# Eight of the 24 table units that are turned beside the first feed-forward's output product are turned later, beside the query product

## The reference: two transformer blocks, the second ending in a layer of single experts

```python
def swiglu(x, w_gu, w_down):                      # first_block, ffn1 (d_ff = 2816)
    g, u = jnp.split(x @ w_gu, 2, axis=-1)
    return (jax.nn.silu(g) * u) @ w_down
...
h = h + 0.5 * rmsnorm(swiglu(rmsnorm(h, ffn1_pre_w), ...), ffn1_post_w)
...
def peer(h, p):                                   # the last layer of second_block
    q = (hf @ p['peer_w_q']).reshape(T, 8, 2, 128)
    s = jnp.einsum('thpd,hpnd->thpn', q, p['peer_keys'])
    top_s, top_i = lax.top_k(s, 16)               # and again over the 256 sums
    ...
    act = jax.nn.gelu(jnp.einsum('td,thkd->thk', xb, u_tab[ib]))
    return jnp.einsum('thk,thkd->td', gb * act, v_tab[ib])
```

## Time and profile before

| | us |
|---|---|
| median of 3 runs | 3853.92 (3853.06 to 3856.65) |
| span of the profiled execution | 3844.7 |
| the execution around its span (median less span) | 9.2 |
| TensorE busy in the span | 3560.4 (93%) |
| VectorE busy | 2403.7 (63%) |
| ScalarE busy | 1320.1 (34%) |
| GpSimd busy | 1860.2 (48%) |
| TensorE in the stretch 460:480 | 9.5 of 20 |

### The profile page before, as it was taken

How to read it: one execution, slowest core, us unless ns; L and a number is a source line. 1 busy time by engine, 2 the same in 40 slices (tenths; PEclk the granted TensorE clock), 3 DMA queues, 4 the chain that set the end, 5 groups by cost and what they waited for, 6 DMA issues and landing times. The chain is left out here.

```text
span 3844.7 us, 49787 instructions
## 1 busy us (share of the span) xinstructions
PE 3560.4 (93%) x17547; PEld 3013.0 (78%) x17547; DVE 2403.7 (63%) x4244; ACT 1320.1 (34%) x1795; POOL 1860.2 (48%) x909
## 2 busy tenths in 40 slices
PE   8999897899999899978989899899999999989998
PEld 5777676677787688765667577689999999988898
DVE  4653255422324454156763754569999996999997
ACT  4332234232343322222323344323345553332332
POOL 5766333233244344331334112346566666788775
PEclk9999998999999999988999999999999999999999
DMA  6997944345366365231324223785469998988895
GB/s 245 392 384 258 297 150 136 116 155 173 120 225 223 101 192 170 89 100 59 116 77 137 71 66 107 230 314 166 156 228 351 343 349 292 344 327 342 327 339 196
DMA packets 458130, 813.81 MB, mean 212 GB/s; under 512 B 31544, under 2 KB 308984, under 8 KB 455322
## 3 DMA queue, kind: packets, MB, share of 16 engines
q1 hardware_dynamic: 278416, 436.07, 34.4%
q10 hardware_dynamic: 142666, 241.11, 17.8%
q0 software_dynamic: 36864, 134.23, 9.3%
HBM read 682.84 MB, written 195.56 MB: 228 GB/s over the span
## 5 line engine op out<-in xcount | busy, mean ns | idle before, releaser
L530 POOL TENSOR_TENSOR weights_lo<-weights_raw,weights_hi 128x1024 fp32r<-128x1024 f32 x649 | 1600.3, 2471 | 1913.8 <-ACT weights_hi L1204 1725.8
L606 PE MATMUL bank<-operand_hi,weights_hi 128*128 128x512 f32 (+1 forms) x2856 | 1093.1, 383 | 64.1 <-DVE operand_lo L1885 23.0
L608 PE MATMUL bank<-operand_hi,weights_lo 128*128 128x512 f32 (+1 forms) x2856 | 1063.8, 372 | 0.0
L607 PE MATMUL bank<-operand_lo,weights_hi 128*128 128x512 f32 (+1 forms) x2856 | 1063.5, 372 | 0.0
L1204 ACT ACTIVATE weights_hi<-weights_raw 128x1024 fp32r<-128x1024 f32 x649 | 681.7, 1055 | 828.3 <-PE bank L608 646.2
L606 PEld LDWEIGHTS bank<-operand_hi,weights_hi 128*128 128x128 f32 x2856 | 541.2, 190 | 156.8 <-DVE operand_lo L1885 29.1
L607 PEld LDWEIGHTS bank<-operand_lo,weights_hi 128*128 128x128 f32 x2856 | 541.4, 190 | 74.4 <-issue 6.1
L608 PEld LDWEIGHTS bank<-operand_hi,weights_lo 128*128 128x128 f32 x2856 | 540.4, 189 | 74.9
L606 PE MATMUL bank<-expert_hi,weights_hi 128*128 128x384 f32 x1024 | 356.6, 348 | 51.3 <-DVE expert_lo L2557 49.1
L607 PE MATMUL bank<-expert_lo,weights_hi 128*128 128x384 f32 x1024 | 352.4, 344 | 0.0
L608 PE MATMUL bank<-expert_hi,weights_lo 128*128 128x384 f32 x1024 | 352.0, 344 | 0.0
(11 more groups left out here) (399 smaller groups left out, 5061.7 us busy)
## 6 DMA issues: line engine op xcount, KB each, us to landing
weights_raw<-in_w_ffn_gu SPq DMA_DIRECT2D x132, 512.0 KB, 5.3
expert_table_v<-in_w_peer_out SPq DMA_DIRECT2D x120, 512.0 KB, 5.3
weights_raw<-in_w_peer_ahead SPq DMA_DIRECT2D x120, 512.0 KB, 3.9
weights_raw<-in_w_peer_out SPq DMA_DIRECT2D x120, 512.0 KB, 4.4
expert_table_u<-expert_turned ACTq DMA_DIRECT2D x288, 128.0 KB, 4.4
expert_rows<-in_w_peer_ahead ACTq DMA_DIRECT2D x64, 512.0 KB, 6.2
peer_gates<-gate_stage SPq DMA_DIRECT2D x24, 1024.0 KB, 8.9
expert_gates<-peer_gates ACTq DMA_DIRECT2D x16, 1536.0 KB, 12.1
```

Source lines behind the costliest of these rows:

```text
L530: pool.tensor_tensor(LO[:, slot, :], RAW[:, slot, :], HI[:, slot, :].bitcast(F32), ALU.subtract).then_inc(sem("lo_ready"), 1)
L606: pe.matmul(out, wh, hi(k), start=(k == 0), stop=False)
L607: pe.matmul(out, wh, lo(k), start=False, stop=False)
L608: ins = pe.matmul(out, wl, hi(k), start=False, stop=(k == kc - 1))
```

## The change

The ranges of `TABLE` move: d1 has 16 units instead of 24, q has 40 instead of 32 (so 31 instead of 23 in wq, since wout2 keeps nine), f2 keeps 18. `DOWN_TURNS` says how many turns stand before each of the eight blocks of d1: 3, 3, 3, 3, 2, 2, 0, 0. ScalarE's wait for the last stores of d1 moves from before the eighth square to behind the root. The total number of turns, loads and stores stays 128, 128 and 512.

```diff
-TABLE = {"f1": range(0, 54), "d1": range(54, 78), "f2": range(78, 96), "q": range(96, 128)}
+TABLE = {"f1": range(0, 54), "d1": range(54, 70), "f2": range(70, 88), "q": range(88, 128)}
 WOUT_TURNS = 9
+DOWN_TURNS = [3, 3, 3, 3, 2, 2, 0, 0]
+assert sum(DOWN_TURNS) == len(TABLE["d1"])
@@ scalar, ffn
                     if name == "ffn1":
-                        for _ in range(3):
+                        for _ in range(DOWN_TURNS[m]):
                             save_rows("d1")
                     square(YT[:, m, :], TOK, "block_free", n["freed"] + m + 1)
-                    if name == "ffn1" and m == DC - 1:
-                        for i in range(2):
-                            act.wait_ge(sem(f"table_stored_d1{i}"), 64 * len(TABLE["d1"]) // 2)
@@ scalar, after ffn1
             ffn("ffn1", n["freed"], x_squares)
             root(TOK)
+            for i in range(2):
+                act.wait_ge(sem(f"table_stored_d1{i}"), 64 * len(TABLE["d1"]) // 2)
@@ vector, ffn
-                        for t in range(3 * m, 3 * m + 3):
+                        for t in range(sum(DOWN_TURNS[:m]), sum(DOWN_TURNS[:m + 1])):
                             turn_rows("d1", t)
                         copy_blocks(YT, 1, FC, first=m, scaled=True)
```

## The result

Median 3862.9 us over 8 runs (3856.9 to 3869.3), against 3853.3 over 8 runs of the kernel before on the same chip (3849.8 to 3856.7): the medians differ by 9.6 us, the ratio is 1.003 with a 95% interval of 1.002 to 1.004 (7.7 to 15.4 us). So the changed kernel is slower, by about a quarter of a percent. The prediction said 3864.6, in 3849 to 3874.

What follows compares the result with a forecast made beforehand. TensorE was busy in 3560.4 of 3844.7 us, so changes matter where it stands still or is made to; -8.8 + 17 + 2.5 = +10.7 us on 3853.9 gave 3864.6, range 3849 to 3874.

Steps and rivals of the forecast that it cites:

- First term: End of d1: copies of blocks 6 and 7 wait for TensorE alone, reciprocal earlier; gain 8.8 us, range 7.8 to 9.8.
- Second term: wq: eight added turns wait for rows at the DMA rate, last query copy later; cost 17 us, range 12 to 22.
- The catch-up of four turns: wq before the change: four late turns took 12.92 us, 3.23 us each; called the forecast's weakest point.
- rival 1: wq: the q stage keeps up and only the d1 gain is left, 3845.1 us, faster; chance 0.13.
- Third term: Score products behind wq: TensorE idles some 17 us, then runs at the lower clock; cost 2.5 us, bounds 0 and 4.
- Nothing absorbs it: Behind wq: TensorE and VectorE both begin behind the last query copy, so neither can catch up the 17 us.
- The sum: Whole kernel: -8.8 + 17 + 2.5 = +10.7 us, median 3864.6 us.
- The 9.2 us: Whole kernel: median of runs 3853.92 less span 3844.7, taken to lie outside the span and kept unchanged.
- Two of the signs: Reciprocal of d1 8 to 10 us earlier; last query copy some 8 us later on the clock of the span.
- About a fifth: Share of the forecast's 0.59 (wq cost under 14 us) ending under 3861.6 us, so counted as no change.
- rival 3: wq: the f1 stage's lower rate of 359 GB/s holds, wq cost 28.8 us, time 3876.4 us; chance 0.07.
- The estimate that I drew from it: wq: by the skill page's bound of about 358 GB/s a core, the wq cost would be 27 us.

Runs made afterwards that it cites:

- d1_only: Changed kernel with q's units as before, so eight units are copied unturned (output not the reference's): 3839.4 us, 12 us under before.
- wait_only: Kernel before with only the wait for d1's stores moved behind the root, three turns left beside each block: no change that can be measured.
- q_only: Kernel before with 40 units in q instead of 32, eight being turned twice: 3874.5 us, 22 us above before by the medians.
- six_buffers: Changed kernel with six row buffers in q instead of four: 3859.9 us.
- half_rows: Changed kernel loading only 512 of 1024 columns of q's rows from number 13 on (output not the reference's): 3858.4 us.
- sp_half: Changed kernel with q's row loads from number 13 on issued by SyncE behind its weight loads, and halved (output not the reference's): 3852.1 us.
- sp_loads: Changed kernel with q's row loads from number 13 on issued by SyncE behind its weight loads, at full size: 3866.3 us.

## Why the prediction was right, point by point

**First term (-8.8).** Right, for the reason given: d1_only and wait_only show that the turns did 8 of the 10 us. The term's chain had one row too many: I left the root's table load (1.28 us) on the path, and it moved ahead of the mean. So the chain became 10.0 us shorter, just outside my 7.8 to 9.8. The 8.75 us of the pair of traces lie inside it by luck: TensorE lost 1.3 us within d1 in that one execution (from the first copy to the last matmul 109.8 us, in before 108.5; the granted clock over 345 to 470 was 0.97, in d1_only 0.99), in d1_only it lost nothing, and the gain in A is 10.0 us. Over all seven kernels with 16 turns A is 112.7 us on average, against 122.5, 122.1 and 120.9 in the three with turns up to block 7 (before, q_only, wait_only). TensorE's wait for weights within d1 is no part of it (3.1 us before, 3.0 after). The lower clock behind it lasted 3.9 us as before (483.56 to 487.47).

**Second term (+17).** The mechanism was right, the size low: 19.9 us, inside my 12 to 22. The ends of that range were worked loosely: by the same sum 430 GB/s gives 12.9 us and 3.4 us a turn 20.8; 19.9 lies between these too. A turn took 3.37 us, not 3.23. The catch-up of four turns had no weaker moment in it; over the whole stage the rate by bytes is 34.6 MB in 87.6 us, 395 GB/s, as single turns waited longer (4.80 us between those at 2496.24 and 2501.04). The ceiling itself was as read, 402 to 404 GB/s. In the rivals I had also held the ring of row buffers (3.1 us a turn) against rival 1; six_buffers and the 2.52 us a turn of sp_half with four buffers show that the ring isn't what held the turns. And I had counted ScalarE's issuing for rival 1 (5.4 of 5.5 us); half_rows shows that it takes 6.0 us a block, so that without the ceiling rival 1 would have failed too, on ScalarE's issuing.

**Third term (+2.5).** 2.1 us, by the granted clock, in the place named.

**Nothing absorbs it.** Right: from the first MAX8 to the start of VectorE's last instruction it is 1272.8 us before and 1273.7 after.

**The sum.** +10.7 forecast, +9.6 measured, +13.3 by the distances of one pair of traces, and -10.0 + 19.9 + 2.1 = +12.0 with the first term of d1_only. All of these lie inside the interval of the ratio (+7.7 to +15.4 us). The first term was 1.2 us too small and the second 2.9 too small, with opposite signs, so that the forecast came as near as 1 us is in part luck. The 9.2 us that I kept as lying outside the span don't lie there: an execution is 1.8 us longer than its span (3867.1 against 3865.3 here), and the rest is that the profiled execution of before was a short one. In a difference this drops out. Two of the signs were given on the clock of the span, where the shifts of earlier stages come in: the reciprocal came 4.8 us earlier and the last query copy 17.6 us later, and only the distances show the 8 to 10 us and the size of the second term. "About a fifth" of the forecast's 0.59 is also not the 0.15 that I then added to "same", which is a quarter.

**The page of the skill.** The Trainium skill (DMA: Bandwidth & Descriptors, section "Where 436 GB/s comes from") holds that about 358 GB/s bind between device memory and SBUF. The rows of wq (402 to 404 GB/s in five kernels, for 15 to 60 us) disagree, in a run with one core at work. The estimate that I drew from it was also 2 us low: 34.6 MB at 358 GB/s are 96.6 us, so by the way of rival 3 the second term would be 29 us and not 27.

## What to carry to other kernels

Moved transfers cost nothing only where the new stage has bytes to spare: add what the stage moves already and what is added, divide by the highest rate that any of its stretches shows while something waits, and compare with the time of the engine that it lies beside. Here 32 units in q are just that much (26.2 MB behind the fifth turn, 65 us at 403 GB/s, beside 65.5 us), and each unit more costs 2.1 to 2.5 us. Look for the few units that do the harm before you move many: taking the turns off the last block alone, with the wait moved, gave most of the gain without the loss.

When an experiment eases one limit and the time hardly moves, read who issues back to back before you call the theory wrong; and when a queue is given more work, read what it now delivers late, a stage further on.

## What the runs showed of the hardware

- In wq a mix of 512 KB loads, 128 KB stores and weight loads ran at 402 to 404 GB/s and not above, in every kernel that asked for more with ScalarE issuing the row loads, with a DMA share of 1.05 to 1.06; with SyncE issuing them it was 389 GB/s (sp_loads, 2500.43 to 2528.11). It is no limit of the whole kernel: in before, another mix moved 419 GB/s for 15 us (3500 to 3515) at a share of 1.02. What sets it stays open, and the share alone doesn't tell it, since it also read 1.02 at 350 GB/s (half_rows).
- ScalarE needs some 0.5 us for each DMA that it issues in this stage (four in 2.04 to 2.18 us), and as much in d1 of the changed kernel (a median of 0.50 us a store), where the DMA share is 0.75. Five a turn were a limit of their own.
- The granted clock still read 1.00 through a wait of 2.2 us, and fell within the products behind it (0.68). Small fp32 matmuls of 128 columns in a wait of 9.2 us kept it up: the first product behind took 0.47 us and the next 0.39, against 0.77 and 0.63 without.
